# Seven half-size products for eight in a third gated-unit layer, and the modulation rows moved beside two down layers

## What is computed

```python
# first block, last step
hn = rmsnorm(h, g_ffn)
h = h + (silu(hn @ w_gate) * (hn @ w_up)) @ w_down          # D_FF = 2816

# second block
mods = split(silu(c) @ w_ada + b_ada, 9)                    # sh1, sc1, gt1, ... gt3
h = rms_norm(x, g_ffn1) * (1 + sc1) + sh1
x = x + 0.5 * gt1 * swiglu(h, w1_gu, w1_down)
...                                                         # mixing layers with sh2, sc2, gt2
h = rms_norm(x, g_ffn2) * (1 + sc3) + sh3
x = x + 0.5 * gt3 * swiglu(h, w2_gu, w2_down)
```

## Time and profile before

| | us |
|---|---|
| median of 3 runs | 2023.1 |
| lowest, highest | 2022.56, 2024.08 |
| the profiled execution | 2023.45 |
| its span | 2021.6 |

### The profile page before, as it was taken

One profiled execution on the slowest core, in us unless ns is written; L12 is line 12 of the kernel. 1 busy time (PEld: TensorE's weight loads), 2 busy tenths in 40 slices (PEclk: granted clock), 3 DMA queues, 4 the chain that ended last, 5 costly groups with the idle time before them and its releaser, 6 DMA issues.

```text
span 2021.6 us, 30547 instructions
## 1 busy us (share of the span) xinstructions
PE 1998.5 (99%) x10974; PEld 1698.5 (84%) x10974; DVE 1139.0 (56%) x1733; ACT 846.6 (42%) x1443; POOL 854.7 (42%) x396
## 2 busy tenths in 40 slices
PE   9999999999999999999999999999999999999998
PEld 7788788878888888889998888888777888999887
DVE  4666865343888886687770154374552347777111
ACT  4243454344232222456662243224663246666322
POOL 3345223314454454544444434443234445444443
PEclk9999999999999999999999999999999999999999
DMA  6353212213665676333333325433212333333331
GB/s 218 93 147 115 74 54 83 84 33 124 228 192 193 190 265 219 100 100 104 104 104 96 112 75 158 115 94 93 64 63 84 93 94 94 105 104 104 95 103 62
DMA packets 67094, 234.08 MB, mean 116 GB/s; under 512 B 7617, under 2 KB 9025, under 8 KB 66497
## 3 DMA queue, kind: packets, MB, share of 16 engines
q1 hardware_dynamic: 66288, 231.77, 37.0%
q10 hardware_dynamic: 720, 1.15, 0.2%
HBM read 225.02 MB, written 2.10 MB: 112 GB/s over the span
## 4 chain that ended last, share of the span: by engine, by line
PE 94%; DVE 3%; ACT 1%; issue 1%; POOL 0%; POOLq 0%; DVEq 0%; ACTq 0%
PE bank L2139 15%; PE bank L2140 15%; PE bank L2145 15%; PE bank L2318 6%; PE bank L2322 6%; PE bank L2319 6%; PE bank L2264 5%; PE bank L2263 5%; PE bank L2269 5%; PE bank L2113 1%; PE bank L2115 1%; PE bank L2114 1%; PE bank L2437 1%; PE bank L2445 1%; PE bank L2438 1%
## 5 line engine op out<-in xcount | busy, mean ns | idle before, releaser
L541 POOL TENSOR_TENSOR wlo<-raw,whi 128x1024 fp32r<-128x1024 f32 x269 | 669.9, 2491 | 939.8 <-ACT whi L635 939.6
L635 ACT ACTIVATE whi<-raw 128x1024 fp32r<-128x1024 f32 x269 | 283.8, 1056 | 515.5 <-PE bank L2269 241.4
L2139 PE MATMUL bank<-xh,whi 128*128 128x512 f32 x1052 | 414.1, 394 | 0.5 <-DVE proj L1359 0.3
L2140 PE MATMUL bank<-xl,whi 128*128 128x512 f32 x1052 | 409.7, 389 | 0.0
L2145 PE MATMUL bank<-xh,wlo 128*128 128x512 f32 x1024 | 252.7, 389 | 0.0
L2139 PEld LDWEIGHTS bank<-xh,whi 128*128 128x128 f32 x1052 | 197.5, 188 | 45.2 <-issue 3.7
L2140 PEld LDWEIGHTS bank<-xl,whi 128*128 128x128 f32 x1052 | 197.5, 188 | 40.8 <-issue 0.7
L2145 PEld LDWEIGHTS bank<-xh,wlo 128*128 128x128 f32 x1024 | 192.2, 188 | 40.1
L2264 PE MATMUL bank<-hl,whi 128*128 (+1 forms) x480 | 186.7, 389 | 0.0
L2263 PE MATMUL bank<-hh,whi 128*128 (+1 forms) x480 | 186.7, 389 | 0.0
L1632 DVE CUSTOM_DVE_ANT_0 xn<-ada_w,csilu 128x1024 f32<-128x1024 f32 x72 | 136.9, 1902 | 4.2 <-DVE mods L1639 2.3
(11 more groups left out here) (388 smaller groups left out, 3902.6 us busy)
## 6 DMA issues: line engine op xcount, KB each, us to landing
raw<-units SPq DMA_DIRECT2D x341, 512.0 KB, 3.6
ada_w<-ada_rows SPq DMA_DIRECT2D x72, 512.0 KB, 4.5
h<-x_t SPq DMA_DIRECT2D x8, 256.0 KB, 4.6
out_t<-h SPq DMA_DIRECT2D x8, 256.0 KB, 2.1
raw<-units SPq DMA_DIRECT2D x4, 256.0 KB, 4.1
mem_in<-mem_t SPq DMA_DIRECT2D x1, 1024.0 KB, 11.3
turned_q<-proj SPq DMA_DIRECT2D x4, 256.0 KB, 6.6
dec<-decays SPq DMA_DIRECT2D x4, 256.0 KB, 7.0
```

The costliest lines, as they stand in the source:

```text
L541: pool.tensor_tensor(wlo[:, j % 2 * UNIT:(j % 2 + 1) * UNIT], raw[:, j * UNIT:(j + 1) * UNIT], whi[:, j % 2 * UNIT:(j % 2 + 1) * UNIT].bit ...
L635: act.activation(whi[:, v % 2 * UNIT:(v % 2 + 1) * UNIT], raw[:, slot * UNIT:(slot + 1) * UNIT], ACT.Copy).then_inc(hi_ready, 1)
L2139: mm(bank[:, 0:n], wh, chunk(rhs[0], t, n), start=t == 0, stop=False)
L2140: mm(bank[:, 0:n], wh, chunk(rhs[1], t, n), start=False, stop=False)
```

## The change

- `gu` joins `FAST`: its first 4 pairs stay plain and the other 18 take the seven-product form. Its inputs are not normed ahead, so the factor `rstd` is applied to the results. VectorE scales the right half of gate from PSUM (`right_by_tokens`) and the left half behind its sum (a second, half-wide instruction that waits for the first), ScalarE takes silu of both, and GpSimd multiplies silu's whole result with `rstd` once more (`gate_by_tokens`), which stands for the scaling of up. VectorE's product of gate and up (`whole_product`) now waits for GpSimd, and stands behind the fourth weight sum.
- Ahead of the loop GpSimd adds the 8 input chunks (`x32`) during `xo`, and VectorE forms the input sums ahead of the norm's reciprocal.
- The modulation rows leave `gu`: 9 rounds stand beside `down` and 9 beside `down1` (`units_and_rows`), `csilu` is loaded and silu'd at each, since the loop's `s4_hi` lies in its place. `scale_rows` then makes the factors of the first norm behind the first nine, those of the other two behind the last.
- `w_t3_low` gets a buffer of its own, and `down` uses the banks in the order of the other down layers.

```diff
-FAST = {"gu1": 0, "gu2": 1}
+FAST = {"gu": 0, "gu1": 1, "gu2": 2}
...
+            def units_and_rows(u, name, rows, end):
+                sp.wait_ge(unit_used, L[name].u0 + 2 * FC)
+                sp.dma_start(csilu[:, :], c_rows).then_inc(c_in, 16)
+                sp.wait_ge(five_done, GN_BEFORE + 5 * FAST_PAIRS * (FAST[name] + 1))
+                for _ in range(ADA_N):
+                    load_ada(rows // ADA_N, rows % ADA_N, rows < ADA_N)
+                    rows += 1
+                while rows < end or u % 4:
+                    load_unit(u, u % 4)
+                    u += 1
+                    for _ in range(2):
+                        if rows < end:
+                            load_ada(rows // ADA_N, rows % ADA_N)
+                            rows += 1
...
+                def gate_by_tokens(g, r):
+                    pool.wait_ge(acted, ACTED[name] + 5 + g)
+                    pool.tensor_tensor(chunk(tmp, r), chunk(tmp, r), rstd[:, :], ALU.mult).then_inc(gate_rescaled, 1)
...
                     if not final:
                         gate_first(i, g + 1, 1 - r)
+                    if name == "gu" and not start:
+                        gate_by_tokens(g - 1, 1 - r)
                     up_second(i, g, r)
...
                 def gate_right(g, r):
-                    act.activation(right(chunk(tmp, r)), left(banks[GATE_BANK[r]]), func).then_inc(acted, 1)
+                    if name == "gu":
+                        act.wait_ge(gate_scaled, 5 + g)
+                        act.activation(right(chunk(tmp, r)), right(chunk(tmp, r)), func).then_inc(acted, 1)
...
+                def right_by_tokens(g, r):
+                    last = isinstance(g, int) and g == G - 1
+                    dve.wait_ge(five_done, GN_BEFORE + 5 * (G * k + g) + (5 if last else 6))
+                    tt(right(chunk(tmp, r)), left(banks[GATE_BANK[r]]), right(rstd), ALU.mult).then_inc(gate_scaled, 1)
...
+                def whole_product(g, r):
                     dve.wait_ge(up_left, GN_BEFORE + G * k + g + 1)
+                    if name == "gu":
+                        dve.wait_ge(gate_rescaled, 5 + g)
                     dve.wait_ge(acted, a0 + 5 + g)
                     tt(fast_product, fast_product, chunk(tmp, r), ALU.mult).then_inc(prod, 1)
...
+                    if name == "gu":
+                        tt(left(chunk(tmp, r)), left(banks[LEFT_BANK]), part1, ALU.add).then_inc(left_added, 1)
+                        dve.wait_ge(left_added, 5 + g)
+                        tt(left(chunk(tmp, r)), left(chunk(tmp, r)), left(rstd), ALU.mult).then_inc(gate_left, 1)
...
-            pairs("gu", (hh, hl), ada_dots)
+            fast_pairs("gu", (hh, hl))
...
                 def gate_first(g, r):
-                    if isinstance(g, int) and g == 0:
-                        pe.wait_ge(acted, a0 + 3)
+                    if name == "gu":
+                        pe.wait_ge(gate_scaled, 3 + g)
...
+            fast_products("gu")
             down("down", HALVES["gu"] + FC)
```

More of the change, by code:

```diff
@@ L464, in _ @@
             turn(1, turned_k, proj, PR["rk"], 4)
[L465 to L486, removed]
             def fast_units(name):
@@ L597, in fast_lows @@
                 over_pairs(pool, body)
-            u = 2
-            for name in FAST:
+                if name == "gu":
+                    gate_by_tokens(FAST_PAIRS - 1, 1)
+            xo0, u0 = L["xo"].u0, L["gu"].u0
+            low_parts(2, xo0 + 3)
+            for c in range(7):
+                low_part(xo0 + c + 3, (xo0 + c + 3) % 4)
+                whole_inputs("gu", range(c, c + 1))
+            whole_inputs("gu", range(7, C))
+            for v in range(u0 + 2, u0 + PLAIN):
+                low_part(v, v % 4)
+            fast_lows("gu")
+            u = u0 + 2 * FC
+            for name in ("gu1", "gu2"):
                 u0 = L[name].u0
@@ L745, in body @@
                         high_part(lay.u0 + u0, i, j + 1)
+                        if first and j == 1 and norm in ("ffn1_2", "mix_2"):
+                            act.wait_ge(c_in, 16 + 16 * SHIFTED[norm])
+                            act.activation(csilu[:, :], csilu[:, :], ACT.Silu).then_inc(csilu_done, 1)
                 repeat(act, 2, body)
@@ L879, in body @@
                         act.wait_ge(five_done, n5 + 1)
+                    if name == "gu":
+                        t_high(i, g, 4)
+                    if not start:
                         gate_right(g - 1, 1 - r)
-                    t_high(i, g, 4)
+                    if name != "gu":
+                        t_high(i, g, 4)
                     if not start:
@@ L1200, in _ @@
             memory_out_high(3)
-            act.wait_ge(c_in, 16)
-            act.activation(csilu[:, :], csilu[:, :], ACT.Silu).then_inc(csilu_done, 1)
             high_part(L["xo"].u0, 0, 2)
@@ L1598, in body @@
                         form_low(2)
+                    if name == "gu" and not start:
+                        right_by_tokens(g - 1, 1 - r)
                     t_low(i, g, 4)
                     if not start:
-                        up_left_and_product(g - 1, 1 - r)
+                        up_left_sum(g - 1)
+                    if name != "gu" and not start:
+                        whole_product(g - 1, 1 - r)
                     if not final:
                         t_last_sum(i + r, g + 1, 1 - r)
+                    if name == "gu" and not start:
+                        whole_product(g - 1, 1 - r)
                     if start:
@@ L1623, in ada_dots @@
                 for j in js:
-                    if first and j == 0:
-                        dve.wait_ge(csilu_done, 1)
-                        dve.wait_ge(kmem_done, C)
-                    elif j == 0:
+                    if not first and j == 0:
                         dve.wait_ge(ada_sum, i)
```

207 lines of the change are left out of this document (132 added, 75 removed).

## The result

The changed kernel takes **2059.9 us** (median of 4 runs, 2058.5 to 2060.6), the kernel before 2023.4 (4 runs beside it): ratio 1.018, 95% interval 1.016 to 1.020, so slower by 1.8%. The forecast was 2064.0. The profiled execution took 2058.5, its span 2056.7.

The account below looks back on a forecast made before the run. TensorE, 99% busy, bounds the kernel before; in gu three port waits make a pair 13.45 us, so 18 pairs take 237.1 against 196.0: +41.1 on 2023.45 gives 2064.5, taken as 2064, range 2036 to 2086 (0.80).

Parts of the forecast that it names:

- The behaviour that decides: VectorE instructions with both inputs in SBUF and GpSimd instructions shut each other out for their whole length; 2.33 us against 0.69.
- the second rival: Two shared waits: gu's left multiply comes first or is not shut out; 12.3 us a pair, 2046; chance 0.17.
- The walk of the pair: Steady pair of gu, timed instruction by instruction from GpSimd's low part of up's second half: 13.45 us, 3.55 of port waits.
- All three races: In gu, GpSimd against VectorE's left multiply, weight sums and product: shared waits of 1.13, about 1.27 and 1.15 us.
- the second shared wait: In gu, GpSimd's low part of the raw half meets the weight sums; VectorE loses about 1.27 us a pair.
- TensorE's pause: In each steady pair of gu TensorE stands still 3.37 us, as it is not last in the ring.
- the prediction's sign: What would show it: TensorE's stretch of gu's 18 pairs is 237 us long with 182 busy.
- The sum: For gu's 18 pairs: 183.2 + 53.9 (16 pairs at 3.37) = 237.1 against 196.0, +41.1 us.
- the ring: Closed chain of waits from one gu pair to the next; 13.45 us, or 9.9 without port waits.
- The parts at nothing: Input sums ahead of gu (bounds 0 to 3 us), rows and loads beside down and down1 (0 to 8): no cost.
- The margin of 5 us at the end of `down`: Modulation rows beside down would end at 822.8, first needed at 827.88: 5 us left.
- The clock: Rival: TensorE's pauses in gu halve its clock, 107 us more, 2171, if the mean is under 0.75; chance 0.05.

Follow-up runs that it names:

- the kernel of 2013.2: Changed kernel with three waits added on GpSimd in gu and GpSimd's multiply by rstd cut in two halves; 2013.2 us, ratio 0.995.
- 2011.0: Changed kernel without any multiply by rstd in the 18 fast pairs of gu; 2011.0 us, ratio 0.994.

## Why the prediction was right

- **What bounds.** It said TensorE at 99% and the question whether VectorE's slack holds the added work. It held the work (the kernel of 2013.2 does all of it) and not the waits.
- **The behaviour that decides.** Read from one pair of rows each way, and shown by four kernels (one wait added, three times, and the left multiply's input in PSUM). It holds for half-wide instructions, which no row showed: 1.42 us for 0.42. What the second rival needed, that they be exempt, is not so. One reading was off: that the two engines hardly meet in `gu1`. Two of GpSimd's three low parts meet VectorE there in every pair (966.82 takes 1.67 us, 969.43 takes 1.75), but VectorE is first each time and keeps its 0.69, and GpSimd's delay is in nobody's way. That is the order which the added waits bring back.
- **The walk of the pair.** 13.45 us were forecast, 12.95 measured (654.90 to 667.91 is 13.01, the pair before it 12.92). From the end of GpSimd's low part (656.05, the 0 of the walk): product's end 0.56 (forecast 0.55), left multiply's end 3.99 (4.0), last low part 5.90 (6.18), first weight sum 6.61 (6.91), right half scaled 9.52 (10.0), GpSimd's multiply from 10.46 (10.95) and to 11.77 (12.2), next zero 13.0 (13.5). All three races fell as the walk had them; the one called close, 2.37 against 2.53, came out at 2.41 against 2.57.
- **The term that was too large** is the middle. Half of the 0.5 us a pair was gone by the last low part: the one ahead of it came 0.12 sooner after the left multiply (4.96 for 5.08), and the last low part follows the right half of up by 0.33, where I had taken 0.49, the distance of `gu1`, in which ScalarE's copy came late; here it was ready at 661.74. Most of the rest is the second shared wait, on which I put the full 1.27, and which measured 1.10.
- **TensorE's pause.** Forecast 3.37 us a pair at full clock. Measured are ten pauses of 2.54 to 2.66 and six of 1.16 to 1.28, because of the clock (below). TensorE is busy for 196.0 us of the 18 pairs, where the prediction's sign said 182; some 12 of the 14 more are the clock (a mean of 0.95 over 232.3 us).
- **The sum.** 237.1 for the 18 pairs against 232.3 measured: 16 x 0.5 = 8 us too much in the steady pairs, some 3 too little at the two ends, where I had let two pairs run on slack. The ends fell short because the ring held from the first pair on (GpSimd's low parts of up's second half at 525.47, 538.24 and 551.10, 12.8 apart). At the start of `down` (717.0 before, 752.79 after) 35.8 us were lost, forecast 41.1. The sum's 2064.5 stands 6.0 over the profiled 2058.5, and 5.3 of that are this term's. The two errors have opposite signs, so part of how near the number came is luck; the count of three waits, which put it there, is not.
- **The parts at nothing.** `down` takes 120.0 and `down1` 119.7 us, TensorE waits in neither, and the kernel with the rows' move alone shows no cost. The margin of 5 us at the end of `down` was 3.7: the rows are scaled by 860.29, which I had left out, and 863.97 is the first instruction that needs them:

```profile
858.04 2.25 DVE L2076 TENSOR_TENSOR shift_parts<-mods,shift_parts 128x8 fp32r<-128x8 f32 x1
863.97 4.29 DVE L1381 SCALAR_TENSOR_TENSOR xl<-h,gmod,xh 128x512 fp32r<-128x512 f32 x4 [3.67 <-ACT xh L720]
```

- **The clock.** It was a rival at 0.05, to cost 107 us if the mean fell under 0.75. It fell to 0.95 and cost nothing that can be seen. Four stretches of 2 us, two pauses and what follows each:

```profile
646.00:648.00 2.00, 0.00 (x0) 0.00 (x0) 1.67 (x2) 0.90 (x3) 0.79 (x1) 1.00 0.21 31
649.00:651.00 2.00, 2.00 (x11) 2.00 (x11) 1.97 (x3) 0.55 (x2) 1.27 (x1) 0.50 0.27 111
659.00:661.00 2.00, 1.10 (x10) 0.90 (x8) 1.64 (x2) 0.93 (x3) 0.76 (x1) 1.00 0.24 37
662.00:664.00 2.00, 2.00 (x19) 2.00 (x19) 1.97 (x3) 1.13 (x3) 1.30 (x1) 1.00 0.25 98
```

After the 2.63 us pause (645.77 to 648.40) TensorE is granted half, 1.2 GHz, for some 3.4 us, and then full, 2.4 GHz, again. What it loses shortens its next pause to 1.27, after which the grant stays full. This is not regular: of the ten long pauses seven are followed by such a stretch, three are not (those that end at 570.65, 635.46 and 700.27, as long as the others), and none of the six short ones is. The pair with the slow stretch is no longer than the one before it, which has full clock throughout: 12.98 us (648.40 to 661.38) against 12.94 (635.46 to 648.40). The slow stretch takes up time in which TensorE would have waited, as the prediction had the pause take the clock up. "TensorE: Matmul & The Clock Gate" of the Trainium skill, section "Part 1: The HAM clock gate", has activity lift the clock and its absence lower it; the rows agree with that direction.

## What to carry over

Before work is put on a free VectorE or GpSimd, list for both engines which instructions have two inputs in SBUF, and at what moment of the loop each starts; the busy share (62% and 42% here) does not tell it. Where two of them meet and VectorE is the one that waits, two cures worked here, for 17 to 18 us each: an input in PSUM, or a wait on GpSimd so that VectorE's instruction goes first. The wait costs nothing as long as what GpSimd makes is wanted later. Taking work off GpSimd is not a cure by itself: the next instruction comes earlier. Before you delay a GpSimd instruction, ask who waits for its result and also who waits for the buffer that it reads: the next load may.

## What the hardware showed that I had not expected

- A half-wide instruction on GpSimd (128x256) takes 0.74 us, more than half of the whole one's 1.30, while VectorE's take 0.42 and 0.69.
- A full-wide VectorE instruction caught behind GpSimd ends 0.55 to 0.56 us behind it, the half-wide one 0.29 (659.75 to 660.04).
- The granted clock of TensorE fell and rose seven times in the 18 pairs, after some pauses of 2.6 us and not after others, and the length of a pair doesn't show it. What a fallen clock costs where TensorE is the bound, no run here tells: the kernels of 2013.2 and 2011.0 hardly pause and are granted 1.00.
